# Second layer's modulation summed by the vector engine inside the feed-forward stages; the mixers' attention loop one step deeper, on four score banks

## What is computed

```python
for layer in range(2):
    mx = split(silu(c) @ ada_w[layer] + ada_b[layer], 9)         # modulation, one row of 9216
    mc = split(silu(c_ctx) @ ada_w[layer] + ada_b[layer], 9)
    x   = x   + 0.5 * mx[2] * swiglu(modulate(rms_norm(x), mx[0], mx[1]), ffn1_gu, ffn1_down)
    ctx = ctx + 0.5 * mc[2] * swiglu(modulate(rms_norm(ctx), mc[0], mc[1]), ffn1_gu, ffn1_down)
    hx, hc = modulate(rms_norm(x), mx[3], mx[4]), modulate(rms_norm(ctx), mc[3], mc[4])
    # projections; attention of 8 heads, latents over 512 keys, context over 256;
    # a pooling mixer; a 2-D Fourier mixer; then the output projection
    x = x + mx[5] * mixers(hx, hc)
    x = x + 0.5 * mx[8] * swiglu(modulate(rms_norm(x), mx[6], mx[7]), ffn2_gu, ffn2_down)
    # the context gets the same mixers and second feed-forward, in the first layer only
```

## Time and profile before

| | us |
|---|---|
| median of 3 runs | 2355.08 (2350.37 to 2357.55) |
| profiled execution | 2349.65 |
| its span, first to last instruction | 2347.9 |
| PE busy | 2275.5 (97%) |
| DVE busy | 1060.8 (45%) |
| ACT busy | 695.0 (30%) |
| POOL busy | 198.3 (8%) |

### The profile page before, as it was taken

The page is one execution under the profiler, slowest core; times in us unless marked ns, Lnnn a source line. Parts: engine busy times, 40 slices in busy tenths (PEclk is TensorE's granted clock), DMA queues, the critical chain, the costliest instruction groups (busy, mean ns, idle before and its releaser), DMA issues.

```text
span 2347.9 us, 32138 instructions
## 1 busy us (share of the span) xinstructions
PE 2275.5 (97%) x13844; PEld 1829.4 (78%) x13844; DVE 1060.8 (45%) x1626; ACT 695.0 (30%) x950; POOL 198.3 (8%) x195
## 2 busy tenths in 40 slices
PE   7999999999999999999999999999999999989998
PEld 6778975555478888899459888888888888848998
DVE  5676534333364333352446333335433334446554
ACT  5444331111142212232444221213212222344333
POOL 2111210000010000120112000012000003012002
PEclk9999998999999999999999999999999999999999
DMA  9775887999953243232843323323323323444573
GB/s 291 259 266 181 287 305 292 420 421 420 398 151 97 80 120 90 75 96 77 319 142 90 91 86 110 100 75 97 108 80 109 95 73 115 152 169 133 165 203 110
DMA packets 371515, 407.81 MB, mean 174 GB/s; under 512 B 10841, under 2 KB 342094, under 8 KB 350126
## 3 DMA queue, kind: packets, MB, share of 16 engines
q1 hardware_dynamic: 356174, 326.07, 42.2%
q0 software_dynamic: 14896, 79.09, 9.2%
q10 hardware_dynamic: 304, 0.59, 0.1%
HBM read 404.66 MB, written 1.05 MB: 173 GB/s over the span
## 4 chain that ended last, share of the span: by engine, by line
PE 86%; DVE 7%; ACT 3%; DMA 2%; issue 1%; SPq 0%; POOL 0%; DVEq 0%; ACTq 0%
PE B L1739 23%; PE B L1741 22%; PE B L1740 22%; PE B L2118 6%; PE B L2138 3%; PE B L2088 2%; DMA HF<-in_ada_w 2%; PE B L1860 2%; PE B L2076 2%; ACT T L1667 1%; DVE LO L669 1%; DVE SM L1232 1%; DVE R L680 1%; DVE HF L1025 1%; DVE T L1245 1%; DMA XS<-in_ctx 1%
## 5 line engine op out<-in xcount | busy, mean ns | idle before, releaser
L1739 PE MATMUL B<-hH,HI 128*128 128x512 f32 (+1 forms) x1936 | 659.1, 340 | 14.0 <-DVE hL L1013 7.0
L1740 PE MATMUL B<-hL,HI 128*128 128x512 f32 (+1 forms) x1936 | 653.8, 338 | 0.0
L1741 PE MATMUL B<-hH,LO 128*128 128x512 f32 (+1 forms) x1936 | 653.7, 338 | 0.0
L669 DVE TENSOR_TENSOR LO<-RAW,HI 128x2048 fp32r<-128x2048 f32 (+3 forms) x218 | 443.8, 2038 | 121.2 <-ACT HI L1323 111.4
L1323 ACT ACTIVATE HI<-RAW 128x2048 fp32r<-128x2048 f32 (+3 forms) x218 | 368.6, 1692 | 356.6 <-PE B L1741 276.8
L1739 PEld LDWEIGHTS B<-hH,HI 128*128 128x128 f32 x1936 | 368.8, 190 | 60.0 <-DVE LO L669 11.9
L1741 PEld LDWEIGHTS B<-hH,LO 128*128 128x128 f32 x1936 | 368.9, 191 | 39.4
L1740 PEld LDWEIGHTS B<-hL,HI 128*128 128x128 f32 x1936 | 369.0, 191 | 38.4 <-issue 0.2
L1124 DVE TENSOR_TENSOR T<-B,T 128x512 f32<-128x512 f32 (+1 forms) x88 | 55.0, 625 | 492.4 <-PE B L1741 492.4
L1741 PE MATMUL B<-aH,LO 128*128 128x512 f32 (+1 forms) x770 | 269.3, 350 | 0.0
L1739 PE MATMUL B<-aH,HI 128*128 128x512 f32 (+1 forms) x770 | 269.0, 349 | 0.0
(11 more groups left out here) (353 smaller groups left out, 2631.8 us busy)
## 6 DMA issues: line engine op xcount, KB each, us to landing
RAW<-in_ffn_w_gu SPq DMA_DIRECT2D x176, 512.0 KB, 5.0
W<-in_w SPq DMA_DIRECT2D x78, 1024.0 KB, 11.5
HF<-in_ada_w POOLq DMA_DIRECT2D x48, 1024.0 KB, 7.8
W2T<-in_w SPq DMA_DIRECT2D x39, 1024.0 KB, 11.9
RAW<-in_w_in SPq DMA_DIRECT2D x60, 512.0 KB, 5.0
RAW<-in_ffn_w_down SPq DMA_DIRECT2D x56, 384.0 KB, 3.7
RAW<-in_ffn_w_down SPq DMA_DIRECT2D x56, 320.0 KB, 4.2
ADW<-in_ada_w POOLq DMA_DIRECT2D x16, 1024.0 KB, 10.8
```

The source lines that it names most:

```text
L669: V.tensor_tensor(LO[s][:, :words], RAW[s][:, :words], HI[t.hi[s]][:, :words].bitcast(F32), ALU.subtract).then_inc(lo_done[s], 1)
L1739: mm(o, wh, xh, start=first, stop=False, **more)
L1740: mm(o, wh, xl, start=False, stop=False, **more)
L1741: return mm(o, wl, xh, start=False, stop=last, **more)
```

## The change

The second layer's modulation no longer runs as matmuls against the weights. POOL loads pieces of 128 rows by 1024 columns (`MADW`, two places, 72 pieces of 512 KB). DVE multiplies a piece by the silu value of its row, a scalar per partition, and adds it to one accumulator of 1024 columns for each of the two vectors (`mod_sum`: two instructions per piece). When 8 pieces are summed, PE adds over the partitions (`mod_sums`: 8 matmuls of 256 columns with the constant `PICK`), ACT copies (`mod_copy`), PE turns the result (`mod_turn`: 2 matmuls) and DVE adds the bias (`mod_read`). Three of the nine such sums fall into each of the first three feed-forwards. All of `ada` leaves the mixers. In the attention loop the product with V and the low part now belong to pair u-3, the transposes to pair u-2; scores use four banks, the probabilities six tiles. The table `POOL` shares its place with `MADW` and is loaded a second time for the second layer.

```diff
-        FILL = (0, 2, 3, 3)
-        SCORE_BANKS, PROBS = (0, 1, 5), (T[0], T[1], T[4], T[5])
+        SCORE_BANKS, PROBS = (0, 1, 5, 6), (T[0], T[1], T[4], T[5], R[0], R[1])
 # POOL
+            def mod_weights(n0, n1):
+                for n in range(n0, n1):
+                    m, k = n // KT, n % KT
+                    if n >= 2:
+                        pool.wait_ge(*mod_used(n - 2))
+                    pool.dma_start(MADW[n % 2][:], a["ada_w_2"][1][k * P:(k + 1) * P, MOD_W * m:MOD_W * (m + 1)])\
+                        .then_inc(ada_loaded[n % 2], 16)
...
+            units = MODS_PER_FFN * KT
+            mod_weights(2, units)
+            pool_tables(units)
             after_ffn(2)
-            pool.wait_ge(E["pf_ready"], 4)
-            ada_weights(ADA_UNITS, ADA_UNITS + 3 * KT)
+            pool.wait_ge(E["pool_done"], 2)
+            mod_weights(units, units + 2)
             even_squares_in_turn()
+            mod_weights(units + 2, 2 * units)
             after_ffn(2)
+            mod_weights(2 * units, 3 * units)
+            pool_tables(3 * units)
             after_ffn(2)
-            pool.wait_ge(E["v_ready"], 2)
-            ada_weights(ADA_UNITS + 3 * KT, 2 * ADA_UNITS)
 # DVE
+            def mod_sum(n):
+                k = n % KT
+                ve.wait_ge(ada_loaded[n % 2], 16 * mod_used(n)[1])
+                if n > 0:
+                    ve.wait_ge(*mod_used(n - 1))
+                for v in range(2):
+                    c = CS[:, k, v:v + 1]
+                    if k == 0:
+                        ins = V.tensor_scalar(MACC[v][:], MADW[n % 2][:], c, None, ALU.mult)
+                    else:
+                        ins = V.scalar_tensor_tensor(MACC[v][:], MADW[n % 2][:], c, MACC[v][:], ALU.mult, ALU.add)
+                ins.then_inc(ada_used[n % 2], 1)
...
                         if j > 0 or half > 0:
                             prep(FFN_CHUNKS[j + 1])
+                        if f is not None and half == 1 and j == 1:
+                            mod_read(MODS_PER_FFN * f + 1)
+                        if f is not None and 1 <= j <= KT:
+                            mod_sum(KT * (MODS_PER_FFN * f + 2 * half) + j - 1)
                         products()
...
+                    if f is not None:
+                        mod_read(MODS_PER_FFN * f + 2 * half)
...
                             prep(words)
+                        if f is not None and half == 0 and i < KT:
+                            mod_sum(KT * (MODS_PER_FFN * f + 1) + i)
                         products()
 # PE
+            def mod_sums(m):
+                claim(6, "ada_copied", len(ADA_GROUPS) + m + 1)
+                pe.wait_ge(*mod_used(KT * (m + 1) - 1))
+                w = MOD_W // COL_TILES
+                for v in range(2):
+                    for j in range(COL_TILES):
+                        ins = mm(B[6][CT_W * j:CT_W * (j + 1), 0:w], PICK[:, v, :], MACC[v][:, w * j:w * (j + 1)],
+                                 start=(v == 0), stop=(v == 1))
+                ins.then_inc(E["mod_summed"], 1)
+
+            def mod_turn():
+                got("ada_copied")
+                claim(7, "mod_read")
+                o = B[7][:, 0:2 * KT].rearrange("p (j c v) -> p j c v", j=COL_TILES, v=2)
+                for c in range(KT // COL_TILES):
+                    ins = mm(o[:, :, c, :], MADT[:, c * P:(c + 1) * P], ASEL[:].rearrange("p (j v) -> p j v", v=2),
+                             start=True, stop=True)
+                ins.then_inc(E["ada_done"], 1)
...
                     for j in range(FT_HALF):
+                        if f is not None and j == FT_HALF - 1:
+                            mod_sums(MODS_PER_FFN * f + 2 * h)
+                        elif f is not None and h == 1 and j == 0:
+                            mod_sums(MODS_PER_FFN * f + 1)
+                        elif f is not None and h == 1 and j == 1:
+                            mod_turn()
...
+                    if f is not None:
+                        mod_turn()
 # PE, mixers: ada(FILL[1]), ada(FILL[2]), ada(FILL[3]) are gone; in the attention loop
-                for u in range(len(pairs) + 2):
+                for u in range(len(pairs) + 3):
...
-                        banks = [SCORE_BANKS[(2 * u + c) % 3] for c in range(2)]
+                        banks = [SCORE_BANKS[(2 * u + c) % 4] for c in range(2)]
...
-                    if u >= 2:
-                        h, q0, k0, nk = pairs[u - 2]
+                    if u >= 3:
+                        h, q0, k0, nk = pairs[u - 3]
...
-                    if 1 <= u <= len(pairs):
-                        h, q0, k0, nk = pairs[u - 1]
+                    if 2 <= u <= len(pairs) + 1:
+                        h, q0, k0, nk = pairs[u - 2]
...
-                    if mix_finish(l, u) is not None:
-                        ada_finish(1, mix_finish(l, u))
-                    if mix_unit(l, u):
-                        ada(1)
```

More of the change, by code:

```diff
@@ L241, in build @@
         DFT = at(61, "DFT", [P, 2, TB, S])
+        MACC = [at(45 + 4 * v, f"MACC{v}", [P, MOD_W]) for v in range(2)]
+        MADW = [at(53 + 4 * i, f"MADW{i}", [P, MOD_W]) for i in range(2)]
         TRIG = at(65, "TRIG", [P, 2, S])
@@ L1113, in into, with ffn @@
                     norm(l, shift, scale, 1, [], {})
-            def ffn(l, gate, n):
+            def ffn(l, gate, n, f=None):
                 sets = range(n // S)
+                if f == 0:
+                    ve.wait_ge(E["cs_ready"], 2)
+                    link(V.memset(PICK[:], 0.0))
+                    for v in range(2):
+                        V.memset(PICK[:, v, v:v + 1], 1.0)
                 for half in range(2):
@@ L1532, in _, with ffn @@
             norm(0, 0, 0)
-            def ffn(n, more):
+            def ffn(n, more, f=None):
                 for half in range(2):
@@ L1539, in ffn @@
                             prep(FFN_CHUNKS[j + 1])
+                        if f is not None and (j == FT_HALF - 1 or half == 1 and j == 0):
+                            mod_copy()
                         got("gate_done")
@@ L1923, in _ @@
                 if h in (0, 4):
-                    ada_finish(0, 0 if h == 0 else 1)
+                    ada_finish(0 if h == 0 else 1)
                 ada(HEAD_UNITS[h])
@@ L1951, in _ @@
             head_probs(HEADS - 1)
-            ada_finish(0, 2)
+            ada_finish(2)
             head_out(HEADS - 1)
@@ L2062, in _ @@
                 .then_inc(E["base_done"], 1)
-            ada_finish(0, 3)
+            ada_finish(3)
             ada(4)
```

141 lines of the change are left out of this document (71 added, 70 removed).

## The result

On the same chips the kernel before took 2352.7 us in the median of 11 runs (2350.12 to 2357.75) and the changed kernel 2358.84 (2354.32 to 2366.55). The ratio is 1.0027, with a 95% interval of 1.0016 to 1.0037: 6 us slower, within the 0.3% that the prediction called no change, 2.8 us above the forecast of 2356 and inside its range. The forecast of the time is somewhat closer than the forecast of the change: it started from a median of 2355.08, 2.4 us above the one measured here, and added 1.2 where 6 came out.

What follows compares the result with a forecast made beforehand. PE was taken to bound the feed-forwards, and DVE and ACT the attention-loop steps. Terms -18.3 + 3.0 + 13.5 + 3 = +1.2 us on the median 2355.08 gave about 2356, range 2348 to 2367.

Steps and rivals of the forecast that it cites:

- Fills removed: Mixers, ahead of the attention loops: taking out PE's `ada` units saves 7.5 and 10.8 us, sum -18.3, bounds -17 and -19.3.
- PE work in the feed-forwards: First three feed-forwards: nine `mod_sums` at 1.0 us and nine `mod_turn` add +13.5 us, bounds +12 and +17.
- DVE, ACT, POOL and the loads there: Feed-forwards: DVE's sums, some 180 us, ACT's copies and POOL's loads are hidden and cost nothing.
- Loop steps: Attention loops: a step over 512 keys stays at 4.36 us; three small gains give -2.0 us.
- Drain: End of each attention loop: one more distance between two products with V, +5.0 us, bounds +4.5 and +5.3.
- The clock: Start of each attention loop: one dip of PE's clock over one to two steps, +3 us, bounds 0 and +10.
- first rival: Attention loops: PE's clock swings throughout, and two output projections begin low; +12 in place of +3, 2365 us; chance 0.20.
- second rival: Attention loops: depth and bank shorten the step from 4.36 to 4.0 us, no dip; 2346 us; chance 0.12.
- third rival: Feed-forwards: DVE is late and PE waits 2 us each, 3 to 5 times; +8, 2363 us; chance 0.07.
- the ring on DVE and ACT: Attention loop: a 512-key step's chain of waits goes ACT, DVE, DVE, DVE, ACT, never PE; 4.36 us.

Runs made afterwards that it cites:

- the filled run: The changed kernel with products that nobody reads added on PE between scores and PV product in the attention loops: 2353.15 us, ratio 0.9999 to the kernel before.
- after: The kernel with the whole change made, against the kernel before: 2358.84 us in the median, 2366.55 in the profiled execution.
- the reordered kernel: The changed kernel with split, next pair's maxima, then scaling on DVE, and copies ahead of exponentials on ACT: 2324.99 us, ratio 0.9880.
- depth two: The changed kernel with its attention loops one step shallower (PV of u-2, transposes of u-1), four score banks kept: 2351.24 us, ratio 0.9992.
- ACT's half of the reordering: The changed kernel with only ACT's copies of u-3 and u-2 moved ahead of the exponentials of u: 2348.23 us, ratio 0.9983.

## Why the prediction was right, and where its terms were not

Gains and costs nearly cancelled, as forecast, but not as closely: 6 us more in the medians where 1.2 was forecast. Two terms were too small, the clock above all. By its own steps:

- **Fills removed**, predicted -18.3: the rotation's start to the Fourier product is 7.9 and 11.0 us shorter, 18.9 in all, with the short waits at the Fourier products that were forecast (0.69 and 0.47 above). Right. (That half of the fills of mixers(1) was waiting, as I wrote, was misread: PE's three waits there are 0.63, 1.43 and 1.42 us of 11.7. The term doesn't use it.) The other 1.6 of mixers(0) in the table lie ahead of the rotation, and that stage varies (54.9 to 56.6 over the kernels with the change's loops).
- **PE work in the feed-forwards**, predicted +13.5, bounds 12 to 17: measured +15.2, and the run without the products gives all of it back. `mod_sums` was priced right at 1.0 and `mod_turn` about right (0.45 for 0.5); left out were the 0.09 before and the 0.11 after `mod_sums`, where the next product starts late. 9 x 1.65 is 14.9.
- **DVE, ACT, POOL and the loads there**, predicted nothing: the run without them is the same. A piece takes 2 x 1.279 us, 2.6, between the bounds.
- **Loop steps**, predicted 4.36 unchanged and 2.0 us of small gains: the steps are unchanged, and at full clock (the filled run) the two loops' steps are 1.6 and 0.5 us shorter than before, 2.1. Right. In after itself the second loop's steps are 1.0 longer, by the clock.
- **Drain**, predicted +5.0 with bounds 4.5 and 5.3: 6.9 - 4.8 and 10.9 - 7.6, that is 5.4 at full clock, after the fillers' price is taken off, a tenth over the upper bound. Right, as one more distance between two PVs in each loop (1.99 and 3.30 in the reordered kernel, 5.3 in all).
- **The clock**, predicted +3 and one dip of one or two steps per loop, bounds 0 and 10: about 8.1 in the profiled execution. This is the term that was mis-sized, and the place was half wrong. I looked at the start of the loops. There the first loop loses 0.2, since DVE and ACT set its pace, and the second, low from about 2085 to 2099, 1.5. The other 6.4 are paid in the drains and in the output projections, which begin at the clock that the drain leaves. The output projections were among the first rival's terms (about 1.5 each) and not among the forecast's; the drains were nowhere. The term varies between executions: in the run without sum products, whose loops are those of after, the second loop took 67.7 us instead of 70.6. What decides between the two isn't shown. The low output projection of the first loop comes from the missing units (it is there at depth two as well), what is low in the second came with the depth.
- **The first rival** (the clock swings through both loops) came halfway in size and not in kind. Its deciding point, low in two or more steps, was reached in the second loop; but the clock rose within the loop and stayed at 1.00 in the steady steps, with PE busy 3.2 of 4.36 us. The Trainium skill, "TensorE: Matmul & The Clock Gate", section "HAM oscillation — how this bites in real kernels", which was its ground, tells of a loop whose waits are longer than its bursts. These steps are the other way round, 3.2 us of work to 1.2 of waiting, so the description doesn't reach them, and "by that rule this rival is the forecast" went further than the page; the clock in the trace, 1.00, agrees with it. What lowered the clock were the pauses at the two ends of a loop. The rival's swings are real all the same: the two kernels with the maxima ahead and one PV bank, where PE pauses 1.88 us at a stretch before every PV, show the clock at 0.50 several times in one loop.
- **The second rival**, a step of 4.0 without the low part in its ring, gave the number exactly: ACT's half of the reordering makes it, and what I held against it, ACT's order, is what stood in its way.
- **The third rival**, DVE late, didn't come: PE waited for DVE's low parts of the down weights once, 1.4 us in the last feed-forward, which has no sums; the run without DVE's sums waits 1.7 there. (Its time should read 2364: 2355.08 + 1.2 + 8.)

The terms together give -18.9 + 15.2 - 2.1 + 5.4 + 8.1 = +7.7 where I had +1.2; the clock is 5.1 of the difference and the insertions 1.7. The table has 8.1, with the variable ends of the neighbouring stages in it, and the medians about 6, so in the usual execution the clock probably costs some 2 us less than in the profiled one. That is an estimate; the mean granted clocks on record point the same way (0.978 in the profiled execution, 0.981 in the median of the 11, against 0.985 in the median at depth two and 0.988 with the fillers).

What the sum didn't hold is the larger point. I read that the ring on DVE and ACT sets the step and that "a deeper PE side or a fourth bank lets nothing start earlier". True of the change as it is. But the depth is what two reorderings need (for the bank that is shown at depth two alone), and these are worth more than five times the change's own difference.

## What to carry to other kernels

When a pipeline's step is set by a ring between engines, write down the ring with every instruction that stands in program order between its members, and break it before adding depth. Here depth and a bank brought nothing by themselves and cost a longer drain; the order that breaks the ring needed them, and the same order without them made the kernel 11 to 49 us slower. A new order has rings of its own: add those up too. Work that is taken from PE where PE waits anyway may have kept its clock up, and a longer drain is a longer row of pauses: ask what starts next at the lower clock.

## What the runs showed of the hardware

- A stretch with PE busy 2.11 of 4 us at the end of a loop was followed by the granted clock at 0.50 and by an output projection with products every 0.43 us instead of 0.23; with products nobody reads in PE's pauses the clock was 1.00 there and the kernel 0.28% faster.
- In a loop with a PE pause of 1.88 us in every step of 5.06, the granted clock went between 1.00 and 0.50 several times; with pauses of 1.18 in steps of 4.36 it stayed at 1.00.
- A group of sixteen records of 128x256, column-tiled, between ordinary products cost 0.09 us before and 0.11 after it beyond its own 1.00; one of four records of 128x8 cost 0.09 after its own 0.36.
- DVE took 1279 ns for 1024 elements of multiply-and-add with two tensors read, and 747 ns for a multiply by the same kind of scalar without the second tensor.
